# First stage of a streaming layer: products of ones ahead of the data, squares on GpSimd, sums inside the last row, a third block in other banks

## What is computed

```python
def rmsnorm(x, g):
    xf = x.astype(jnp.float32)
    y = xf * lax.rsqrt(jnp.mean(xf * xf, axis=-1, keepdims=True) + EPS)
    return (y * g.astype(jnp.float32)).astype(x.dtype)
...
def memory_kv(mem, g, w_k, w_v):
    m = rmsnorm(mem, g)
    B, M, _ = m.shape
    return (m @ w_k).reshape(B, M, MEM_HEADS, MEM_HD), (m @ w_v).reshape(B, M, MEM_HEADS, MEM_HD)
...
def trunk_layer(x, pos, past, mem_k, mem_v, p):
    B, T, _ = x.shape
    h = rmsnorm(x, p['g_mix'])
    z = h @ p['w_in']
    cq, ckv, kpe, rq, rk, rv, rg, sq, sk, sv = jnp.split(z, IN_SPLIT_POINTS, axis=-1)
...
```

## Time and profile before

| | us |
|---|---|
| median of 3 runs | 1723.16 |
| lowest, highest | 1722.9, 1723.59 |
| span of the profiled execution | 1725.7 |
| TensorE busy in it | 1688.8 |
| VectorE busy | 1079.9 |
| ScalarE busy | 539.6 |
| GpSimd busy | 494.8 |

### The profile page before, as it was taken

The page is one execution under the profiler, slowest core; times in us unless marked ns, Lnnn a source line. Parts: engine busy times, 40 slices in busy tenths (PEclk is TensorE's granted clock), DMA queues, the critical chain, the costliest instruction groups (busy, mean ns, idle before and its releaser), DMA issues.

```text
span 1725.7 us, 26449 instructions
## 1 busy us (share of the span) xinstructions
PE 1688.8 (98%) x10467; PEld 1561.3 (90%) x10467; DVE 1079.9 (63%) x1443; ACT 539.6 (31%) x959; POOL 494.8 (29%) x221
## 2 busy tenths in 40 slices
PE   7999999999999999999999999999999999999997
PEld 7999889776667789998899999999999999999997
DVE  6964457697666765537587656565655656565568
ACT  6210121487656551205233121211213021120235
POOL 0772022000000213430233424243333334243331
PEclk9999999999999999999999999999999999999999
DMA  5222021411112414416211111111111111111113
GB/s 216 86 74 80 23 66 40 134 36 62 62 50 78 138 54 131 133 47 257 84 50 37 37 49 36 49 36 49 36 48 37 49 36 41 44 36 49 37 47 110
DMA packets 35005, 119.28 MB, mean 69 GB/s; under 512 B 4976, under 2 KB 8016, under 8 KB 32496
## 3 DMA queue, kind: packets, MB, share of 16 engines
q1 hardware_dynamic: 32624, 108.76, 19.2%
q10 hardware_dynamic: 2304, 9.44, 1.6%
HBM read 100.73 MB, written 15.17 MB: 67 GB/s over the span
## 4 chain that ended last, share of the span: by engine, by line
PE 92%; DVE 3%; ACT 2%; issue 1%; DMA 0%; POOL 0%; DVEq 0%; SPq 0%; ACTq 0%
PE scores L1996 36%; PE bank L1996 34%; PE scores L2224 3%; PE bank L2281 3%; PE scores L2069 2%; PE bank L2305 2%; PE scores L2018 1%; PE bank L2005 1%; PE scores L2246 1%; PE bank L2335 1%; PE bank L2339 1%; PE bank L2298 1%; PE bank L2575 1%; PE bank L2018 1%; DVE kbuf L1643 1%
## 5 line engine op out<-in xcount | busy, mean ns | idle before, releaser
L877 POOL TENSOR_TENSOR w_hi<-w_raw,zero 128x1024 fp32r<-128x1024 f32 x96 | 188.5, 1963 | 1137.1 <-PE bank L1996 477.7
L1996 PE MATMUL scores<-act_hi,w_hi 128*128 128x384 f32 x960 | 324.2, 338 | 0.0
L1996 PE MATMUL scores<-act_hi,w_lo 128*128 128x384 f32 x960 | 322.6, 336 | 0.0
L1996 PE MATMUL scores<-act_lo,w_hi 128*128 128x384 f32 x960 | 322.5, 336 | 0.0
L880 POOL TENSOR_TENSOR w_lo<-w_raw,w_hi 128x1024 fp32r<-128x1024 f32 x96 | 251.7, 2622 | 7.6
L1924 DVE TENSOR_TENSOR x<-bank,x 128x384 f32<-128x384 f32 x216 | 120.4, 558 | 103.6 <-PE bank L1996 103.6
L1996 PEld LDWEIGHTS scores<-act_hi,w_hi 128*128 128x128 f32 x960 | 180.5, 188 | 0.6 <-issue 0.2
L1996 PEld LDWEIGHTS scores<-act_lo,w_hi 128*128 128x128 f32 x960 | 180.5, 188 | 0.3 <-issue 0.2
L1996 PEld LDWEIGHTS scores<-act_hi,w_lo 128*128 128x128 f32 x960 | 180.5, 188 | 0.0
L1996 PE MATMUL bank<-act_hi,w_hi 128*128 128x384 f32 x528 | 177.9, 337 | 0.0
L1996 PE MATMUL bank<-act_hi,w_lo 128*128 128x384 f32 x528 | 177.4, 336 | 0.0
(11 more groups left out here) (356 smaller groups left out, 3137.0 us busy)
## 6 DMA issues: line engine op xcount, KB each, us to landing
w_raw<-wstream SPq DMA_DIRECT2D x108, 512.0 KB, 3.6
x_blk<-xT ACTq DMA_DIRECT2D x8, 576.0 KB, 4.7
x_mid<-x_blk ACTq DMA_DIRECT2D x8, 576.0 KB, 3.1
x<-x_mid SPq DMA_DIRECT2D x4, 1152.0 KB, 5.4
z<-cache_k SPq DMA_DIRECT2D x4, 1024.0 KB, 5.2
z<-cache_v SPq DMA_DIRECT2D x4, 1024.0 KB, 7.1
mk_c<-mk_c SPq DMA_DIRECT2D x4, 1024.0 KB, 11.6
mv_c<-mv_c SPq DMA_DIRECT2D x4, 1024.0 KB, 13.6
```

The source lines that it names most:

```text
L877: pool.tensor_tensor(w_hi[:, k], w_raw[:, k], zero[:].unsqueeze(2).to_broadcast([P, KB, P]), ALU.add).then_inc(w_rounded, 1)
L1996: mm = pe.matmul(out, w[:, k, at + kb], x(kb), start=first and kb == 0 and n == 0, stop=last and kb == n_kb - 1 and n == 2)
```

## The change

It has these parts, all in the first stage but one:

- TensorE begins with 16 products of `ones` by `ones` (128 columns) into bank 7, which nobody reads.
- SyncE loads two rows of both weight blocks ahead of row 1 of `x`, the six others behind it. ScalarE and VectorE split these two rows of both blocks in one instruction each.
- TensorE takes row 0 by parts: six products hi x hi as soon as both are rounded, then six hi x lo, then six lo x hi.
- GpSimd squares rows 2, 3 and 4 of `x` and adds them up in `x_square`; ScalarE squares five rows. VectorE adds GpSimd's sum last.
- GpSimd squares the memory and adds its eight rows in three halvings; TensorE sums one row in place of eight. These nine instructions stand ahead of GpSimd's first weight split.
- ScalarE's first, unread instruction is a Sqrt in place of a Copy; memory's root comes straight behind those of `x`.
- The two long sums of `x` stand between the two blocks of row 7, the short one and memory's behind the next chunk, and two chunks follow.
- The third block of columns goes into banks 6, 7 and 2, and memory's products wait for two of its evacuations.
- The store of `conv_new` counts on the semaphore of the other last stores.

```diff
+N_FIRST = 2
+POOL_ROWS = (2, 3, 4)
+ACT_ROWS = [kb for kb in range(KB) if kb not in POOL_ROWS]
+X_SQUARES = 2 * len(POOL_ROWS) - 1
+N_WARM = 16
...
 def in_bank(n, c):
 
+    if n == 2:
+        return (6, 7, 2)[c]
     return (0, 1, 4)[c] if n in RET_BLOCKS else (6, 7, 1)[c] if n == NZ - 2 else 3 * (n % 2) + c
...
+        x_square = Region(off_b, 2 * ROW)("x_square", [P, 2, T])
...
             load_x(0)
-            load_weights(0)
-            load_weights(1)
-            for i in range(1, len(X_PARTS)):
+            for k in range(2):
+                load_rows(k, 0, N_FIRST, w_first_in)
+            load_x(1)
+            for k in range(2):
+                load_rows(k, N_FIRST, KB, w_loaded[k])
+            for i in range(2, len(X_PARTS)):
                 load_x(i)
...
+            for n, kb in enumerate(POOL_ROWS):
+                pool.wait_ge(x_loaded[[first <= kb < last for first, last in X_PARTS].index(True)], 16)
+                if n >= 2:
+                    pool.wait_ge(pool_squares, 2 * n - 1)
+                pool.tensor_tensor(x_square[:, min(n, 1)], x_in[:, kb], x_in[:, kb], ALU.mult).then_inc(pool_squares, 1)
+                if n:
+                    pool.wait_ge(pool_squares, 2 * n)
+                    pool.tensor_tensor(x_square[:, 0], x_square[:, 0], x_square[:, 1], ALU.add).then_inc(pool_squares, 1)
+
+            pool.wait_ge(m_loaded, 16)
+            pool.tensor_tensor(m_sq[:], m_in[:], m_in[:], ALU.mult).then_inc(pool_squares, 1)
+            for n, half in enumerate((4, 2, 1)):
+                pool.wait_ge(pool_squares, X_SQUARES + n + 1)
+                pool.tensor_tensor(m_sq[:, 0:half], m_sq[:, 0:half], m_sq[:, half:2 * half], ALU.add).then_inc(pool_squares, 1)
 
             for slot in range(2, 16):
...
             act.wait_ge(setup_done, 2)
-            act.activation(unread[:], eps[:], ACT.Copy)
+            act.activation(unread[:], eps[:], ACT.Sqrt)
             act.wait_ge(consts_in, 16)
-            for i, (first, last) in enumerate(X_PARTS):
-                act.wait_ge(x_loaded[i], 16)
-                for kb in range(first, last):
-                    if kb < KB - 1:
-                        round_block(kb)
-                    if kb == 0:
-                        for rows in ((0, 1), (1, KB)):
-                            for k in range(2):
-                                round_first(k, *rows)
-                    else:
-                        square_block(kb - 1)
-            square_block(KB - 1)
-            round_block(KB - 1)
-            act.wait_ge(setup_done, 2)
+            round_block(0)
+            round_first()
+            round_block(1)
+            for k in range(2):
+                round_rest(k)
+            round_block(2)
+            square_block(0)
+            round_block(3)
+            square_block(1)
+            round_block(4)
+            for kb in range(5, KB):
+                round_block(kb)
+                square_block(kb)
             roots(Q_X, D, rstd)
+            roots(Q_MEM, D, m_rstd, MEM)
             act.wait_ge(m_loaded, 16)
-            act.activation(m_sq[:], m_in[:], ACT.Square).then_inc(m_squared, 1)
...
+            dve.wait_ge(pool_squares, X_SQUARES)
+            dve.wait_ge(x_summed, len(ACT_ROWS))
+            dve.tensor_tensor(sumsq[:], sumsq[:], x_square[:, 0], ALU.add).then_inc(x_summed, len(POOL_ROWS))
...
+            def input_first_row():
+
+                for n, (w, x, ready) in enumerate(((w_hi, act_hi, (x_rounded, w_first_rounded)), (w_hi, act_lo, (x_split,)),
+                                                   (w_lo, act_hi, (w_first_split,)))):
+                    for made in ready:
+                        pe.wait_ge(made, 1)
+                    for k in range(2):
+                        for c in range(NCH):
+                            pe.matmul(bank[3 * k + c][:, 0:CH], w[:, k, 0], x[:, 0, frames(c)], start=n == 0, stop=False)
...
             def memory_sums():
-                pe.wait_ge(m_squared, 1)
+                pe.wait_ge(pool_squares, X_SQUARES + 4)
                 pe.wait_ge(sum_used, Q_MEM - 1)
-                for kb in range(KB):
-                    mm = pe.matmul(bank[6 + Q_MEM % 2][:, 0:MEM], ones[:], m_sq[:, kb], start=kb == 0, stop=kb == KB - 1)
-                mm.then_inc(sum_ready, 1)
+                pe.matmul(bank[6 + Q_MEM % 2][:, 0:MEM], ones[:], m_sq[:, 0], start=True, stop=True).then_inc(sum_ready, 1)
...
-            for kb in range(KB - 1):
-                input_rows(kb)
+            for _ in range(N_WARM):
+                pe.matmul(bank[7][:, 0:P], ones[:], ones[:], start=True, stop=True)
+            input_first_row()
+            for kb in range(1, KB - 1):
+                pe.wait_ge(x_split, kb + 1)
+                for k in range(2):
+                    if kb == N_FIRST:
+                        pe.wait_ge(w_split, k + 1)
+                    input_row(kb, k)
+            pe.wait_ge(x_split, KB)
+            input_row(KB - 1, 0)
             pe.wait_ge(x_summed, KB)
-            sums(Q_X, ones, sumsq)
-            input_rows(KB - 1)
+            for n in range(2):
+                input_sums(n)
+            input_row(KB - 1, 1, (0,))
+            input_sums(2)
             memory_sums()
+            input_row(KB - 1, 1, (1, 2))
...
-                    pe.wait_ge(sum_used, Q_CKV + 3)
+                    pe.wait_ge(sum_used, (Q_X + 3, Q_MEM + 1)[c] if n == 2 else Q_CKV + 3)
```

93 lines of the change are left out of this document (55 added, 38 removed).

## The result

The changed kernel takes **1736.22 us** (1734.63 to 1738.29), the kernel before 1723.12 in the same session: 1.0071 times as long, 95% interval 1.0059 to 1.0084, or 13.1 us more. The profiled execution of the changed kernel spans 1736.5 us. Both profiled executions are long ones: that of before spans 1725.7 us, where executions at its usual 1723.4 us span 1721.6, and that of the changed kernel is the slowest of its four.

What follows compares the result with a forecast made beforehand. TensorE, busy 98%, was taken as the bound, handing first-stage delay on one for one. Third block at 52.4 instead of 43.6, +8.8 us on 1723.16, gave 1732.0 us; range 1726.0 to 1737.0, forecast 70%.

Steps and rivals of the forecast that it cites:

- the page's letter: First stage: VectorE and GpSimd exclude each other for whole instructions, no 0.13 us hand-over given back; 2.7 us more, +11.5.
- The start: TensorE's first rows: first product at 7.85 instead of 9.14 us, row 1 done at 14.1 instead of 18.2; row 2 waits.
- The series sum: First stage from 12.7 us: VectorE's 16.0 and GpSimd's 21.9 us add up, less hand-overs 35.2; last addition ends about 48.
- the square: GpSimd's square of one row of x, 1152 columns: priced at 2.61 us, as a two-input instruction.
- the lower bound of 2.1: GpSimd's square priced by w_hi instead: 2.1 us for 1152 columns, third block at 50.0, +6.4 us (1729.6).
- The end of the stage: After row 7: GpSimd's two weight splits start at 48.0, the third block at 52.4 instead of 43.6, +8.8 us.
- The roots without a table load: ScalarE's Sqrt table load moves into the wait for x, taking 1.28 us off the path at no cost.
- Rivals 1 and 2: First stage: engines overlap after all, 1719.3 us, 7%; or only some pairs exclude each other, 1723 to 1728, 9%.
- Rival 3: First stage: TensorE's clock falls in the new gaps and lasts into row 6; 1733.8 to 1735.3, say 1734.5 us; 12%.
- Nothing there is late: Behind the third block's start, to about 80 us: evacuations, banks and memory's products cause no wait; priced at nothing.

Runs made afterwards that it cites:

- run 5: The changed kernel without its 16 products of ones at TensorE's start: 1737.64 us.
- runs 7 to 9: The kernel before with 44 or 22 extra products ahead of the third block, or nine tiny GpSimd memsets at its start: 1732.01, 1727.49, 1727.48 us.
- run 6: The changed kernel with GpSimd's nine first-stage squares and additions replaced by memsets of the same tiles, leaving out those squares: 1724.01 us.
- run 12: The changed kernel with eight more products of ones ahead of rows 3, 4 and 6 on TensorE: 1737.11 us.
- run 9: The kernel before with nine memsets of a 128x1 tile, which nobody waits for, at the start of GpSimd's program: 1727.48 us.
- run 10: The changed kernel with four memsets of a 128x1 tile on GpSimd behind its wait near 600 us: 1733.84 us.
- runs 7 and 8: The kernel before with 44 and with 22 extra TensorE products ahead of the third block: 1732.01 and 1727.49 us.
- run 2: The kernel before with only the squaring moved to GpSimd; loads, order of sums and banks as before: 1745.56 us.
- run 11: The changed kernel with no squaring on GpSimd, two square buffers, additions laid better and VectorE halving memory's squares: 1719.22 us.

## Why the prediction was right, and where it was not

The sign and the cause of the first loss were right: GpSimd's squares and VectorE's work exclude each other, and the work of both adds up. 1736.2 lies in the range (1726 to 1737), 4.2 us above the forecast of 1732.0 and outside its own range of 1729.5 to 1734. That the wide range holds it is partly luck: its upper part stood for a loss of clock in the first stage and for the page's letter, and what filled it is a loss at 600 us that the prediction doesn't have.

- *The start.* First product 7.85, row 0 to 11.0, row 1 to 14.1 predicted; 8.19, 11.39 and 14.5 measured. Row 2 at 16.6 against 16.58: the gain was lost there, as said, and run 5 shows that it doesn't matter how.
- *The series sum*, the term that decides. Rows 3 to 6 at 23.5, 30.9, 36.5 and 42.4; measured 22.89, 29.81, 34.61 (its split had ended at 34.43) and 40.30. Last addition to 48.1; measured 46.15. The mechanism held and the term was 2 us too large, though GpSimd began 0.5 us later than the 12.7 assumed. Mis-sized was the square: I took 2.61 us from a row with two full inputs, but the first was over 1.9 us after its start (VectorE's `act_lo`, asked for at 14.38, ended at 16.52, so it began to work at 15.1), and that is near the lower bound of 2.1, from w_hi's 1.89 us for 1024 columns. Measured +7.7 lies between that bound (+6.4) and the forecast (+8.8); against the starts of runs 7 to 9 it is 8.3 to 9.4, so the forecast of the stage was nearer than this one trace says. By the letter of the Trainium skill's page SBUF — State Buffer, as the prediction prices it, +11.5, it would have been too much.
- *The end of the stage.* GpSimd's two splits set the third block, as predicted, in 4.35 us. They were to start at 48.0 behind the last addition; they started at 46.92, let go by row 7 of block 0, which the slow row 6 had made late.
- *The roots without a table load*: right, none stands there.
- *Rivals 1 and 2*: out, by rows of 3 to 4 us in the changed kernel and by run 6.
- *Rival 3*, the clock in the gaps: its mechanism is there (rows 3, 4 and 6 begin slowly), its price isn't. It named 1.8 to 3.3 us beyond the forecast's stage; run 12 gives 0.6, since TensorE then waits for VectorE and GpSimd anyway. The forecast came nearer to the median with rival 3's figure (1734.5) only by accident.
- *"Nothing there is late"*: **this step failed.** I asked what lies behind the stage up to 80 us, and of buffers and banks only. At 600 us two engines that exclude each other were in a near tie, 0.06 us apart in the kernel before (600.17 against 600.23), and my own mechanism decides it. GpSimd wakes 0.34 us earlier in every kernel that adds instructions for it to the first stage. That is 4.8 us in the profile of the changed kernel; run 9 shows it alone (+4.0 in the median), run 10 takes it back (2.4 in the median, 4.3 in the span of the profile). 1732.0 less 1.1 (the stage, by its trace) plus 4.8 is 1735.7, and 1736.2 was measured; each of the two terms may be off by 1 to 2 us, so the near agreement of the sum proves little.

Why GpSimd wakes earlier is open. It is not when in the kernel it happens (runs 7 and 8 are shifted and wake at 1.16), nor what its earlier instructions read or how long they take (run 9). An untested rival to their execution is the place of the later instructions in GpSimd's program, which every added instruction moves. Open too is where the executions that were not profiled spend the difference between their times and the traces, up to 4 us for before and for run 2.

## What to carry to other kernels

Before work goes to an idle GpSimd, look at what VectorE does in that stretch: if its instructions read SBUF twice, the two engines' times add up, and idle time on GpSimd is not free time. Squares, sums and splits cost less here with GpSimd left out and the rest laid well (run 11) than on two engines that exclude each other. Search the whole trace for places where both engines meet, not only behind the edit: a start that moves by 0.3 us can turn who comes first there.
